# A hybrid decoder trunk in float32 on one core: weight columns streamed from last to first, with two SBUF regions moved by 128 and 256 bytes

## The chip, the cores and the metric

One core of one Trainium2 chip runs the whole program. The metric is the time on the device in microseconds (us) of one execution. Three runs of the kernel before gave 2097.42, 2097.78 and 2098.17 us; the median is 2097.78.

## The reference

Two pre-norm residual layers and a final RMSNorm, on one sequence of 256 rows of 2048 float32 numbers:

```python
h = x
for i in range(2):
    if i == 0: h = h + stick_breaking_mixer(rmsnorm(h, sb_norm), w_qkv, w_o)   # 16 heads of 128
    else:      h = h + chunked_gmlp_mixer(rmsnorm(h, gm_norm), w_in, v_norm, w_s, b_s, w_o)
    gate, up = split(rmsnorm(h, ffn_norm[i]) @ w_gate_up[i])                    # 2048 -> 2 x 5632
    h = h + (silu(gate) * up) @ w_down[i]                                       # 5632 -> 2048
return rmsnorm(h, final_norm)
```

The weights are 2048 x 6144 (qkv), 2048 x 2048 (attention output), 2048 x 4096 (gMLP input), 2048 x 2048 (gMLP output) and, twice, 2048 x 11264 and 5632 x 2048, all float32. Nearly all of the work is in these eight products.

## The kernel before, in words

**Precision.** Each product is made of three: an operand is split into a high part, rounded to the type float32r, and a low part, the difference. TensorE sums high x high, low x high and high x low.

**Pieces.** The weights are cut into pieces of 256 rows (KP = 2 tiles of 128) by 512 columns (CH). There are 752 of them. A piece takes one slot of a ring of four: SP loads it into `raw`, ACT copies it into `w_hi` (line 348), DVE writes raw minus w_hi into `w_lo` (line 654), and PE uses both. Semaphores `raw_loaded`, `hi_ready`, `lo_ready` and `used` hand a slot on. ACT and DVE run LEAD = 3 pieces ahead of PE.

**PE's work on a piece** is in `piece`. The stationary operand of a matmul is a 128 x 128 tile of the transposed activations (`xT`, or `hid_hi` and `hid_lo` in the region that also holds the attention and gMLP buffers); every matmul has its own load of such a tile, listed as PEld. The moving operand is 128 x 512 of `w_hi` or `w_lo`. Two row tiles, two k tiles and two parts give 8 matmuls on `w_hi` (line 1085); then come 4 on `w_lo` (line 1091). The first eight pieces, while the inputs are still being prepared, and the last four, which are taken row tile by row tile, use the order high-high, high-low, low-high instead (lines 1106 to 1108 and 1343 to 1345).

**Accumulator.** `acc` is four banks of PSUM: two halves, used by turns from one column chunk to the next, of two row tiles of 512 float32 columns each. `acc_at(chunk, rt)` gives one of them.

**Order of the stages.** qkv in four rounds of 24 pieces, with the attention of four heads of the round before put between the pieces (`scores`, line 1156, `values`, line 1176, plain float32); the attention output projection; gate and up of the FFN in eleven rounds of 16 pieces; down in four column chunks of 22 pieces; and the same again with the gMLP in the mixer's place, whose mixing matmuls are at line 1302. On PE the later qkv rounds (line 1215), the residual projections (line 1241), gate/up (line 1257) and the gMLP chunks (lines 1287 and 1307) are hardware loops; the down projections are straight code.

**Addresses.** Tensors follow each other in each partition's memory. `lead_in` is padding that puts the start of `region` at a multiple of 512 bytes from `w_hi`; a stationary tile is 512 bytes of a partition, a moving one 2048. `xT`, `w_hi` and `w_lo` lie at multiples of 512 from each other as well, by their sizes.

Of the kernel before, what the change touches and what calls it, by code (L numbers as in the profile page):

```python
# [5 lines left out]
def hybrid_trunk(nc, x, sb_norm, sb_w_qkv, sb_w_o, gm_norm, gm_w_in, gm_v_norm, gm_w_s, gm_b_s, gm_w_o,  # L6
# [19 lines left out]
    P = 128  # L26
    Q = 32
    S, D = x.shape
    RT = S // P
    F = ffn_w_down.shape[1]  # L30
    CH = 512
    KD = D // P
    KF = F // P
    ND = D // CH
# [8 lines left out]
    RING = 4  # L43
# [26 lines left out]
    def half(v):  # L70
        return v % 2

    ctx = ExitStack()
    with ctx:
        def sb(name, shape, dt=f32):
            return ctx.enter_context(nc.sbuf_tensor(name, shape, dt))
# [6 lines left out]
        xT = sb("xT", [P, KD, 2, S], f32r)  # L83
        xT_hi, xT_lo = xT[:, :, 0], xT[:, :, 1]
        raw = sb("raw", [P, RING, KP, CH])
        w_hi = sb("w_hi", [P, RING, KP, CH], f32r)
        w_lo = sb("w_lo", [P, RING, KP, CH], f32r)
        gate = sb("gate", [P, RT, CH])
        res = sb("res", [P, RT, CH])
# [4 lines left out]
        stop = sb("stop", [P, 3 * P])  # L94
# [9 lines left out]


        used_up_to = nc.lookup_mloc(moments).addr + 32
        lead_in = sb("lead_in", [P, (nc.lookup_mloc(w_hi).addr - used_up_to) % CH // 4])
        region = sb("region", [P, 2 * KF * S])
        R0 = nc.lookup_mloc(region).addr
        assert (R0 - nc.lookup_mloc(w_hi).addr) % CH == 0  # L110
        HB = KF * S * 4

        def at(name, offset, shape, dt=f32):
            return nc.alloc_sbuf_tensor_at(name, shape, dt, offset=R0 + offset)

        hid_hi = at("hid_hi", 0, [P, KF, S], f32r)
        hid_lo = at("hid_lo", HB, [P, KF, S], f32r)
# [24 lines left out]
        acc = ctx.enter_context(nc.psum_tensor("acc", [P, 2 * RT * CH], f32))  # L142
# [57 lines left out]
        def acc_at(chunk, rt):  # L200

            return acc[:, bass.ds(half(chunk) * (RT * CH) + rt * CH, CH)]

        def acc_both(chunk):
            return acc[:, bass.ds(half(chunk) * (RT * CH), RT * CH)].rearrange("p (r n) -> p r n", r=RT)
# [134 lines left out]
        def _(act):  # L340
# [47 lines left out]
            def q_or_k(j, sec, dst, done, t_end):  # L388
                act.wait_ge(used, AT_QKV + j * (3 * PD) + t_end)
                if not isinstance(j, int):  # L390
                    act.wait_ge(qk_turned, j * 2 - 1 + sec)
                for r in range(RT):
                    last = nc.scalar.activation(dst[:, r], acc_at(j * 3 + sec, r), ACT.Copy, scale=rstd[:, 0, r:r + 1])
                last.then_inc(done, 1)
# [676 lines left out]
        def _(pe):  # L1071
            def piece(base, it, per, p, chunk, k0, K, hi, lo, first=False):

                if first and p < 2:
                    pe.wait_ge(half_lo, p + 1)
                elif first:
                    pe.wait_ge(lo_ready, base + it * per + p + 1)
                else:
                    pe.wait_ge(hi_ready, base + it * per + p + 1)
                    for k in range(KP):  # L1080
                        kt = k0 + k
                        for r in range(RT):
                            rs = slice(r * P, (r + 1) * P)
                            for part in (hi, lo):
                                nc.tensor.matmul(acc_at(chunk, r), part[:, kt, rs], w_hi[:, p % RING, k],  # L1085
                                                 start=(kt == 0 and part is hi), stop=False)
                    pe.wait_ge(lo_ready, base + it * per + p + 1)
                    for k in range(KP):
                        kt = k0 + k
                        for r in range(RT):  # L1090
                            last = nc.tensor.matmul(acc_at(chunk, r), hi[:, kt, r * P:(r + 1) * P],  # L1091
                                                    w_lo[:, p % RING, k], start=False, stop=(kt == K - 1))
                    last.then_inc(used, 1)
                    return
                for k in range(KP):
                    kt = k0 + k
                    if first:
                        if p == 0 and k == KP // 2:
                            turn_x0(1, x0_rest_loaded)
                        if p < 2 and k == KP // 2:  # L1100
                            pe.wait_ge(lo_ready, p + 1)
                        pe.wait_ge(n_lo[0], kt + 1)
                    for r in range(RT):
                        rs = slice(r * P, (r + 1) * P)
                        dst = acc_at(chunk, r)
                        nc.tensor.matmul(dst, hi[:, kt, rs], w_hi[:, p % RING, k], start=(kt == 0), stop=False)  # L1106
                        nc.tensor.matmul(dst, hi[:, kt, rs], w_lo[:, p % RING, k], start=False, stop=False)  # L1107
                        last = nc.tensor.matmul(dst, lo[:, kt, rs], w_hi[:, p % RING, k], start=False,  # L1108
                                                stop=(kt == K - 1))
                last.then_inc(used, 1)  # L1110

# [20 lines left out]
            def turn_x0(u, loaded):  # L1132
                pe.wait_ge(loaded, 16)
                for k in (2 * u, 2 * u + 1):
                    for r in range(RT):
                        last = nc.tensor.transpose(tp[0][:, k * S + r * P:k * S + (r + 1) * P],  # L1136
                                                   h[:, r, k * P:(k + 1) * P], ident[:, :])
                last.then_inc(n_turned[0], 1)
# [48 lines left out]
            def first_round():  # L1187
                for t, (sec, p) in enumerate(FIRST):
                    if sec == 2 and p == 0:
                        pe.wait_ge(q_out, 1)  # L1190
                    piece(AT_QKV, 0, 3 * PD, t, sec, p * KP, KD, xT_hi, xT_lo, first=sec == 0)
                    if t < 2:
                        turn_x(1 + t)
                    if t == 5:
                        pe.wait_ge(rows_loaded, 4 * 16)
                        turn_rows(tp[0][:, 0:4 * KD], rows, 4 * KD)

            def qkv_round(j):
                for sec in range(3):
                    for p in range(PD):  # L1200
                        t = sec * PD + p
                        if p == 0:

                            pe.wait_ge((k_out, v_out, q_out)[sec], j + (1 if sec == 2 else 0))
                        piece(AT_QKV, j, 3 * PD, t, j * 3 + sec, p * KP, KD, xT_hi, xT_lo)
                        attention(j - 1, t)
# [5 lines left out]
            turn_x0(0, x_loaded[0])  # L1212
            warm_up(4)
            first_round()
            with pe.Fori(1, ND) as j:
                qkv_round(j)


# [19 lines left out]
            turn(tp[0], res).then_inc(n_turned[1], 1)  # L1238

            def residual_rest(which, base, hi, lo, first):  # L1240
                with pe.Fori(first, ND) as c:
                    for p in range(PD):
                        piece(base, c, PD, p, c, p * KP, KD, hi, lo)
                    pe.wait_ge(res_ready[which], c)
# [23 lines left out]
            for it in range(ND // 2):  # L1268
                for t in range(2 * PF):
                    p = t % PF  # L1270
# [10 lines left out]
            for t, (c, p) in enumerate(PAIR):  # L1281
# [2 lines left out]
                if c == 1 and p == 0:  # L1284
                    pe.wait_ge(res_ready[1], ND)
                piece(AT_GMI, 0, 2 * PD, t, c, p * KP, KD, xT_hi, xT_lo)
            with pe.Fori(2, ND) as c:
                pe.wait_ge(gelu_ready, c - 1)
                for p in range(PD):
                    piece(AT_GMI, c, PD, p, c, p * KP, KD, xT_hi, xT_lo)  # L1290
# [13 lines left out]
                        last.then_inc(mixed_ready, 1)  # L1304

            u_chunk(0, True)
            with pe.Fori(1, ND) as c:
                u_chunk(c, False)
            pe.wait_ge(gelu_ready, 2 * ND - 1)
            for p in range(PD):  # L1310
# [10 lines left out]
            for it in range(ND // 2):  # L1321
                for t in range(2 * PF if it == 0 else ROWWISE):
                    p = t % PF
# [10 lines left out]
            it = ND // 2 - 1  # L1334
            for r in range(RT):
                rs = slice(r * P, (r + 1) * P)
                dst = acc_at(1, r)
                for t in range(ROWWISE, 2 * PF):
                    if r == 0:
                        pe.wait_ge(lo_ready, AT_DOWN[1] + it * (2 * PF) + t + 1)  # L1340
                    for k in range(KP):
                        kt = (t - PF) * KP + k
                        nc.tensor.matmul(dst, hid_hi[:, kt, rs], w_hi[:, t % RING, k], start=False, stop=False)  # L1343
                        nc.tensor.matmul(dst, hid_hi[:, kt, rs], w_lo[:, t % RING, k], start=False, stop=False)  # L1344
                        last = nc.tensor.matmul(dst, hid_lo[:, kt, rs], w_hi[:, t % RING, k], start=False,  # L1345
                                                stop=(kt == KF - 1))
                    if r == RT - 1:
                        last.then_inc(used, 1)
                    elif t == 2 * PF - 1:
                        last.then_inc(first_rows, 1)  # L1350
# [28 lines left out]
```

## Time and profile before

| | |
|---|---|
| median of three runs | 2097.78 us |
| span of the profiled execution | 2097.8 us |
| PE busy | 2088.2 us, 100% |
| PEld busy | 1729.4 us |
| DVE busy | 1430.7 us, 68% |
| ACT busy | 1013.1 us, 48% |
| moved by DMA | 402.47 MB, 192 GB/s on average |

PE is TensorE's matmul side and PEld its loads of stationary tiles, which run beside the matmuls. Matmuls overlap in the pipeline: each is listed with about 0.39 us, so what tells the rate is the difference between two starts, not the duration. The clock granted to TensorE is given as a share of 2.4 GHz.

### The profile page before, as it was taken

The page shows a single profiled execution, that of the slowest core. Times are in us where ns is not written, and L with a number is a line of the kernel's source. Part 1 is how long each engine was busy: PE and PEld are TensorE (multiplying, and loading weights), DVE is VectorE, ACT ScalarE, POOL GpSimd, SP SyncE. Part 2 cuts the span into 40 slices and gives each one's busy share as a digit, 9 for nine tenths or more (in the row PEclk, how much of TensorE's full clock was granted, in tenths as well). Part 3 has the DMA queues.
Part 4 walks back from the last instruction along what each step waited for, and adds up shares of the span by engine and source line. Part 5 has one row for each costly group of instructions (what it writes and reads, how often), then busy time and mean ns, then how long its engine had stood idle before and what let it go on. Part 6 is the DMA issues. An engine that isn't in the chain of part 4 may idle for free.

```text
span 2097.8 us, 27159 instructions
## 1 busy us (share of the span) xinstructions
PE 2088.2 (100%) x9281; PEld 1729.4 (82%) x9281; DVE 1430.7 (68%) x1822; ACT 1013.1 (48%) x1285; POOL 16.4 (1%) x30
## 2 busy tenths in 40 slices
PE   9999999999999999999999999999999999999998
PEld 7888888888888888888888888888888888888887
DVE  6787777867666676665557887877666676664444
ACT  6577765544444444444445444554444444444443
POOL 1000000000000000000000000000000000000000
PEclk9999999999999999999999999999999999999999
DMA  8555554666666666555566665566666666655554
GB/s 264 179 179 170 181 189 167 198 196 192 191 190 198 191 193 195 192 191 196 194 192 209 190 200 183 190 190 201 192 189 198 192 193 194 190 194 198 192 191 150
DMA packets 207419, 402.47 MB, mean 192 GB/s; under 512 B 12336, under 2 KB 13056, under 8 KB 206976
## 3 DMA queue, kind: packets, MB, share of 16 engines
q1 hardware_dynamic: 206496, 398.11, 61.1%
q0 software_dynamic: 688, 3.18, 0.4%
q8 instruction: 36, 0.59, 0.1%
q10 hardware_dynamic: 176, 0.40, 0.1%
q14 instruction: 23, 0.19, 0.0%
HBM read 399.55 MB, written 2.10 MB: 191 GB/s over the span
## 4 chain that ended last, share of the span: by engine, by line
PE 99%; issue 0%; DMA 0%; DVE 0%; ACT 0%; POOLq 0%; POOL 0%; DVEq 0%; SPq 0%
PE acc L1085 64%; PE acc L1091 32%; PE tp L1156 0%; PE tp L1176 0%; PE acc L1106 0%; PE acc L1107 0%; PE acc L1108 0%; PE tp L1302 0%; DMA h<-in_x 0%; PE tp L1116 0%; PE acc L1345 0%; PE acc L1344 0%; PE acc L1343 0%; PE acc L1143 0%; PE tp L1136 0%
## 5 line engine op out<-in xcount | busy, mean ns | idle before, releaser
L654 DVE TENSOR_TENSOR w_lo<-raw,w_hi 128x1024 fp32r<-128x1024 f32 x750 | 916.0, 1224 | 584.9 <-ACT w_hi L348 581.1
L348 ACT ACTIVATE w_hi<-raw 128x1024 fp32r<-128x1024 f32 x750 | 792.9, 1060 | 922.4 <-PE acc L1091 917.2
L1085 PE MATMUL acc<-w_hi,xT 128*128 128x512 f32 x4032 | 998.7, 390 | 0.0
L1085 PEld LDWEIGHTS acc<-w_hi,xT 128*128 128x128 f32 x4032 | 756.0, 188 | 155.9
L1091 PE MATMUL acc<-w_lo,xT 128*128 128x512 f32 x2016 | 539.2, 389 | 0.0
L1091 PEld LDWEIGHTS acc<-w_lo,xT 128*128 128x128 f32 x2016 | 378.6, 188 | 78.5
L1085 PE MATMUL acc<-w_hi,hid_hi 128*128 128x512 f32 x944 | 368.7, 391 | 0.0
L1085 PE MATMUL acc<-w_hi,hid_lo 128*128 128x512 f32 x944 | 367.6, 389 | 0.0
L1091 PE MATMUL acc<-w_lo,hid_hi 128*128 128x512 f32 x944 | 252.5, 389 | 0.0
L1091 PEld LDWEIGHTS acc<-w_lo,hid_hi 128*128 128x128 f32 x944 | 177.3, 188 | 36.7
L1085 PEld LDWEIGHTS acc<-w_hi,hid_hi 128*128 128x128 f32 x944 | 177.3, 188 | 36.8
L1085 PEld LDWEIGHTS acc<-w_hi,hid_lo 128*128 128x128 f32 x944 | 177.3, 188 | 36.4
L853 DVE STREAM_TRANSPOSE tp<-res 32x256 f32<-32x256 f32 x352 | 160.5, 456 | 7.9
L691 DVE STREAM_TRANSPOSE tp<-res 32x256 f32<-32x256 f32 x224 | 102.1, 456 | 4.5
L426 ACT ACTIVATE probT<-prob_blk 32x96 f32<-32x96 f32 x192 | 50.1, 261 | 29.2 <-DVE prob_blk L759 27.0
L533 ACT ACTIVATE gate<-acc,rstd 128x512 f32<-128x512 f32 x44 | 27.9, 685 | 33.2 <-PE acc L1091 33.2
L843 DVE SCALAR_TENSOR_TENSOR res<-acc,rstd,gate 128x512 f32<-128x512 f32 x44 | 31.0, 747 | 9.8 <-PE acc L1091 9.8
L733 DVE STREAM_TRANSPOSE k_t<-k_s 32x256 f32<-32x256 f32 x64 | 27.8, 435 | 1.2
L733 DVE STREAM_TRANSPOSE q_t<-q_s 32x256 f32<-32x256 f32 x64 | 27.9, 435 | 1.2
L862 DVE TENSOR_TENSOR hid_lo<-tp,hid_hi 128x1024 f32 (+1 forms) x22 | 26.8, 1218 | 0.0
L358 ACT ACTIVATE xT<-tp,cols 128x256 fp32r<-128x256 f32 (+1 forms) x48 | 18.9, 475 | 10.1 <-DVE tp L691 10.0
L745 DVE TENSOR_TENSOR_SCAN left<-keep,stop 128x384 f32<-128x384 f32 x16 | 15.3, 955 | 12.0 <-ACT take L410 12.0
(115 smaller groups left out, 477.6 us busy)
## 6 DMA issues: line engine op xcount, KB each, us to landing
raw<-in_ffn_w_gate_up SPq DMA_DIRECT2D x352, 512.0 KB, 4.5
raw<-in_ffn_w_down SPq DMA_DIRECT2D x176, 512.0 KB, 3.6
raw<-in_sb_w_qkv SPq DMA_DIRECT2D x95, 512.0 KB, 4.3
raw<-in_gm_w_in SPq DMA_DIRECT2D x64, 512.0 KB, 4.4
raw<-in_sb_w_o SPq DMA_DIRECT2D x32, 512.0 KB, 4.1
raw<-in_gm_w_o SPq DMA_DIRECT2D x32, 512.0 KB, 4.0
h<-in_x SPq DMA_DIRECT2D x3, 512.0 KB, 7.6
gain_bc<-in_gm_v_norm POOLq DMA_DIRECT2D x1, 1024.0 KB, 6.1
```

The source lines that it names most:

```text
L348: nc.scalar.activation(w_hi[:, p % RING], raw[:, p % RING], ACT.Copy).then_inc(hi_ready, 1)
L358: last = nc.scalar.activation(tile(xT_hi, c * TC + k), tp[0 if m or half(c) == 0 else 1][:, k * S:(k + 1) * S], ACT.Copy, scale=cols[:, ba ...
L426: last = nc.scalar.activation(dst[b * Q:(b + 1) * Q, ns, a], src[a * Q:(a + 1) * Q, ns, b], ACT.Copy)
L533: last = nc.scalar.activation(gate[:, r], acc_at(0, r), ACT.Silu, scale=rstd[:, 1 + 2 * layer, r:r + 1])
L654: nc.vector.tensor_tensor(w_lo[:, p % RING], raw[:, p % RING], w_hi[:, p % RING].bitcast(f32), ALU.subtract).then_inc(lo_ready, 1)
L691: last = nc.vector.transpose(tp[0][b * Q:(b + 1) * Q, :].rearrange("p (k r q t) -> p k r q t", k=TC, r=RT, q=4)[:, :, :, a], res[a * Q:(a ...
L733: last = nc.vector.transpose(dst[b * Q:(b + 1) * Q, :, :].rearrange("p k (r q t) -> p k r q t", r=RT, q=4)[:, :, :, a], src[a * Q:(a + 1) ...
L843: last = nc.vector.scalar_tensor_tensor(out=res[:, r], in0=acc_at(1, r), scalar=rstd[:, 1 + 2 * layer, r:r + 1], in1=gate[:, r], op0=ALU.m ...
L853: last = nc.vector.transpose(tp[1][b * Q:(b + 1) * Q, :].rearrange("p (k r q t) -> p k r q t", k=TC, r=RT, q=4)[:, :, :, a], res[a * Q:(a ...
L862: nc.vector.tensor_tensor(hid_lo[:, ks, :], tp[1][:, :].rearrange("p (k t) -> p k t", k=TC), hid_hi[:, ks, :].bitcast(f32), ALU.subtract). ...
L1085: nc.tensor.matmul(acc_at(chunk, r), part[:, kt, rs], w_hi[:, p % RING, k], start=(kt == 0 and part is hi), stop=False)
L1091: last = nc.tensor.matmul(acc_at(chunk, r), hi[:, kt, r * P:(r + 1) * P], w_lo[:, p % RING, k], start=False, stop=(kt == K - 1))
```

## The change

Every matmul on the weights reads its 512 columns from last to first, and writes the accumulator from last to first. The low ring `w_lo` gets 128 bytes of padding ahead of it (`w_gap`), and `lead_in` puts `region` at 256 bytes past a multiple of 512 from `w_hi`; asserts fix the three distances. The stationary operands are read as before. PE's hardware loops over the later qkv rounds, the residual projections and the gMLP chunks become Python loops, so that PE's code for them is written out; the gate/up loop stays. ACT, DVE, POOL and SP run the same instructions, on the moved addresses.

```diff
         w_hi = sb("w_hi", [P, RING, KP, CH], f32r)
+        w_gap = sb("w_gap", [P, P // 4])
         w_lo = sb("w_lo", [P, RING, KP, CH], f32r)
...
-        lead_in = sb("lead_in", [P, (nc.lookup_mloc(w_hi).addr - used_up_to) % CH // 4])
+        lead_in = sb("lead_in", [P, (nc.lookup_mloc(w_hi).addr + CH // 2 - used_up_to) % CH // 4])
         region = sb("region", [P, 2 * KF * S])
         R0 = nc.lookup_mloc(region).addr
-        assert (R0 - nc.lookup_mloc(w_hi).addr) % CH == 0
+        assert (R0 - nc.lookup_mloc(w_hi).addr) % CH == CH // 2
+        assert (nc.lookup_mloc(xT).addr - nc.lookup_mloc(w_hi).addr) % CH == 0
+        assert (nc.lookup_mloc(w_lo).addr - nc.lookup_mloc(w_hi).addr) % CH == P
...
+        def acc_back(chunk, rt):
+
+            return acc[:, ::-1][:, bass.ds((2 * RT - 1 - rt) * CH - half(chunk) * (RT * CH), CH)]
+
+        def back(t, slot, k):
+
+            return t[:, slot, k, ::-1]
...
-                                nc.tensor.matmul(acc_at(chunk, r), part[:, kt, rs], w_hi[:, p % RING, k],
+                                nc.tensor.matmul(acc_back(chunk, r), part[:, kt, rs], back(w_hi, p % RING, k),
                                                  start=(kt == 0 and part is hi), stop=False)
...
-                            last = nc.tensor.matmul(acc_at(chunk, r), hi[:, kt, r * P:(r + 1) * P],
-                                                    w_lo[:, p % RING, k], start=False, stop=(kt == K - 1))
+                            last = nc.tensor.matmul(acc_back(chunk, r), hi[:, kt, r * P:(r + 1) * P],
+                                                    back(w_lo, p % RING, k), start=False, stop=(kt == K - 1))
...
-            with pe.Fori(1, ND) as j:
+            for j in range(1, ND):
                 qkv_round(j)
...
-                with pe.Fori(first, ND) as c:
+                for c in range(first, ND):
...
-            with pe.Fori(2, ND) as c:
+            for c in range(2, ND):
                 pe.wait_ge(gelu_ready, c - 1)
...
-            with pe.Fori(1, ND) as c:
+            for c in range(1, ND):
                 u_chunk(c, False)
```

The same replacement of `acc_at` by `acc_back` and of the weights by `back(...)` is made in the first round and in the last four pieces.

The order on PE at the start of the later qkv rounds, before: the last piece of the first round and the first two pieces of the loop, with its branch and the instructions that make up its addresses.

```order
L1085 MATMUL acc<-w_hi,xT 128x512 x8
L1091 MATMUL acc<-w_lo,xT 128x512 x4
L1215 UNCONDITIONAL_BRANCH
L1079 ISA
L1085 ISA
L1085 MATMUL acc<-w_hi,xT 128x512 x2
L1085 ISA
L1085 MATMUL acc<-w_hi,xT 128x512 x6
L1091 MATMUL acc<-w_lo,xT 128x512 x4
L1079 REGISTER_ALU
```

And in the changed kernel, PE at the same place: pieces of the second round, up to its first attention step.

```order
L1096 MATMUL acc<-w_hi,xT 128x512 x8
L1102 MATMUL acc<-w_lo,xT 128x512 x4
L1167 MATMUL tp<-kT,qT 128x128
L1167 MATMUL tp<-kT,qT 128x256
L1096 MATMUL acc<-w_hi,xT 128x512 x8
L1102 MATMUL acc<-w_lo,xT 128x512 x4
```

Branch and register instructions are gone from the round; the matmuls and their order are the same (all lines lie 11 further down).

PE at the start of the looped gate/up rounds of the changed kernel:

```order
L1096 MATMUL acc<-w_hi,xT 128x512 x8
L1102 MATMUL acc<-w_lo,xT 128x512 x4
L1268 UNCONDITIONAL_BRANCH
L1090 ISA
L1096 MATMUL acc<-w_hi,xT 128x512 x8
L1102 MATMUL acc<-w_lo,xT 128x512 x4
L1090 REGISTER_ALU
```

This loop stands as before, with one register instruction per piece.

## Rows read from the trace of the kernel before

**Rows 1.** The page: busy us, share of the span, instructions.

```profile
PE 2088.2 (100%) x9281; PEld 1729.4 (82%) x9281; DVE 1430.7 (68%) x1822; ACT 1013.1 (48%) x1285; POOL 16.4 (1%) x30
```

**Rows 2.** Waits of PE: who waited for what, us, times, longest.

```profile
PE acc L1143 <- DVE junk L775: 1.5, 1, 1.5
PE tp L1136 <- DMA h<-in_x: 0.4, 1, 0.4
PE acc L1106 <- DVE w_lo L681: 0.2, 1, 0.2
```

**Rows 3.** Windows: stretch, its length, busy us per engine, clock, DMA share, GB/s.

```profile
887.03:1091.03 204.00, 204.00 (x901) 169.01 (x900) 122.43 (x140) 90.50 (x103) 0.00 (x0) 1.00 0.59 194
```

**Rows 4.** The page: the chain that ended last, by engine.

```profile
PE 99%; issue 0%; DMA 0%; DVE 0%; ACT 0%; POOLq 0%; POOL 0%; DVEq 0%; SPq 0%
```

**Rows 5.** The chain in order of time, gate/up: start us, us, what.

```profile
523.62 1.81 PE acc L1085 x8
...
697.70 1.81 PE acc L1085 x8
```

**Rows 6.** Timeline of PE, attention output projection: start us, us.

```profile
343.04 1.07 PE L1091 MATMUL acc<-w_lo,hid_hi 128*128 128x512 f32 x4
...
356.63 1.07 PE L1091 MATMUL acc<-w_lo,hid_hi 128*128 128x512 f32 x4
```

**Rows 7.** Timeline of PE and PEld, one piece of the down projection.

```profile
1000.14 0.39 PE L1085 MATMUL acc<-w_hi,hid_lo 128*128 128x512 f32 x1
1000.14 0.19 PEld L1085 LDWEIGHTS acc<-w_hi,hid_hi 128*128 128x128 f32 x1
...
1002.86 0.39 PE L1085 MATMUL acc<-w_hi,hid_lo 128*128 128x512 f32 x1
```

**Rows 8.** Timeline of PE, first matmuls of the first round.

```profile
8.70 0.63 PE L1107 MATMUL acc<-w_lo,xT 128*128 128x512 f32 x1
9.13 0.63 PE L1108 MATMUL acc<-w_hi,xT 128*128 128x512 f32 x1
9.55 0.63 PE L1106 MATMUL acc<-w_hi,xT 128*128 128x512 f32 x1
```

**Rows 9.** Timeline of PE, float32 passes of 256 columns in the attention.

```profile
118.21 0.60 PE L1156 MATMUL tp<-kT,qT 128*128 128x256 f32 x2
118.43 0.38 PE L1156 MATMUL tp<-kT,qT 128*128 128x256 f32 x1
118.64 0.38 PE L1176 MATMUL tp<-probT,v_f 128*128 128x256 f32 x1
```

**Rows 10.** Timeline of PE, the piece after an attention step.

```profile
299.07 0.39 PE L1085 MATMUL acc<-w_hi,hid_lo 128*128 128x512 f32 x1
...
300.68 0.62 PE L1091 MATMUL acc<-w_lo,hid_hi 128*128 128x512 f32 x2
```

**Rows 11.** The groups of instructions: the matmuls on the weights, by shape.

```profile
L1085 PE MATMUL acc<-w_hi,xT 128*128 128x512 f32 x4032 | 998.7, 390 | 0.0
L1091 PE MATMUL acc<-w_lo,xT 128*128 128x512 f32 x2016 | 539.2, 389 | 0.0
L1085 PE MATMUL acc<-w_hi,hid_hi 128*128 128x512 f32 x944 | 368.7, 391 | 0.0
L1106 PE MATMUL acc<-w_hi,xT 128*128 128x512 f32 x32 | 13.4, 418 | 0.2 <-DVE w_lo L681 0.2
L1343 PE MATMUL acc<-w_hi,hid_hi 128*128 128x512 f32 x16 | 6.2, 389 | 0.0
```

**Rows 12.** The page: DMA queues, packets, MB, share of 16 engines.

```profile
q8 instruction: 36, 0.59, 0.1%
q14 instruction: 23, 0.19, 0.0%
```

**Rows 13.** Windows of the gate/up stage and the gMLP u half.

```profile
523.62:697.70 174.08, 174.08 (x770) 144.24 (x769) 117.45 (x141) 75.71 (x76) 0.00 (x0) 1.00 0.65 193
1220.00:1290.00 70.00, 70.00 (x337) 58.90 (x336) 62.14 (x109) 30.73 (x33) 0.00 (x0) 1.00 0.57 179
```

More of the change, by code:

```diff
@@ L1104, in piece @@
                         rs = slice(r * P, (r + 1) * P)
[L1105 to L1108, printed above, removed]
+                        dst = acc_back(chunk, r)
+                        nc.tensor.matmul(dst, hi[:, kt, rs], back(w_hi, p % RING, k), start=(kt == 0), stop=False)
+                        nc.tensor.matmul(dst, hi[:, kt, rs], back(w_lo, p % RING, k), start=False, stop=False)
+                        last = nc.tensor.matmul(dst, lo[:, kt, rs], back(w_hi, p % RING, k), start=False,
                                                 stop=(kt == K - 1))
@@ L1336, in _ @@
                 rs = slice(r * P, (r + 1) * P)
-                dst = acc_at(1, r)
+                dst = acc_back(1, r)
                 for t in range(ROWWISE, 2 * PF):
@@ L1342, in _ @@
                         kt = (t - PF) * KP + k
-                        nc.tensor.matmul(dst, hid_hi[:, kt, rs], w_hi[:, t % RING, k], start=False, stop=False)
-                        nc.tensor.matmul(dst, hid_hi[:, kt, rs], w_lo[:, t % RING, k], start=False, stop=False)
-                        last = nc.tensor.matmul(dst, hid_lo[:, kt, rs], w_hi[:, t % RING, k], start=False,
+                        nc.tensor.matmul(dst, hid_hi[:, kt, rs], back(w_hi, t % RING, k), start=False, stop=False)
+                        nc.tensor.matmul(dst, hid_hi[:, kt, rs], back(w_lo, t % RING, k), start=False, stop=False)
+                        last = nc.tensor.matmul(dst, hid_lo[:, kt, rs], back(w_hi, t % RING, k), start=False,
                                                 stop=(kt == KF - 1))
```

## The prediction

> **What bounds the kernel now.** Start with the busy shares of the page: PE, TensorE's matmul side, is busy for 2088.2 us of a span of 2097.8 [rows 1]. A busy matmul engine may still be starved, so the next view is the list of what PE waited for: three waits of 2.1 us in all, by the warm-up, the first transposes and the first round [rows 2]. The granted clock is 1.00 in the wide stretches, which is the 2.4 GHz level, and PE makes up 99% of the chain that ended last [rows 3, 4]. No transfer, no split on ACT or DVE and no semaphore sets the end: it is set by how often TensorE starts a matmul.
>
> So the one number that matters is the spacing of two matmuls. The chain puts a start of an eight-matmul group at 523.62 us and another at 697.70 us [rows 5]; between them lie 64 whole pieces of 12 matmuls (8 with the high weights, 4 with the low), so one piece takes 174.08 / 64 = 2.720 us and one matmul 226.67 ns. The same step shows in the attention output projection, 343.04 to 356.63 us for five pieces [rows 6], and in the first down columns, where twelve matmuls lead from 1000.14 to 1002.86 [rows 7]. The step is the same over high and low weights, over x and hidden activations, and beside a busy DVE or a quiet one.
>
> What could it be? In the first microseconds, before the clock rises, the same matmuls start at 8.70, 9.13 and 9.55 us [rows 8]: 0.425 us apart, and 0.427 is 512 columns at 1.2 GHz, with nothing else. At 2.4 GHz 512 columns are 213.3 ns. The step of 226.67 ns therefore holds **13.3 ns more than the columns**, 32 cycles at 2.4 GHz, paid only at the fast clock. Two rows say that these are no fixed fee of the array. Float32 passes of 256 columns, at two cycles per column also 213.3 ns of array time but with half the bytes per nanosecond, start at 118.21, 118.43 and 118.64 us: 0.215 us each [rows 9]. And just after such passes the main stream is slower than usual: from 299.07 to 300.68 us seven steps take 1.61 us, 0.230 us each, before it falls back to 0.2267 [rows 10]. The same instructions with the same operand shapes thus run at 0.230 or 0.2267, depending on how they stand to something that runs beside them. What runs beside each matmul is the load of the next stationary tile (PEld): it starts within 0.01 us of the matmul and is listed at 0.19 us [rows 7]. It reads 512 bytes of each partition while the matmul reads 2048. My reading, which the trace of before doesn't prove, is that the two reads of the same memory get in each other's way at 2.4 GHz, and that directions and addresses decide how often.
>
> **The change, part by part.** *Descending columns.* All 512-column matmuls on the weights read w_hi and w_lo from last column to first, and write acc from last to first, so the sum lands in the same places. The number is 4032 + 2016 + 3 x 944 + 3 x 32 + 3 x 16 = 9024 [rows 11]. At 226.67 ns they make 2045.4 us; the other 52.4 us (start, transposes, attention, tail) the change doesn't touch. *Addresses.* Before, xT, w_hi, w_lo and the hidden region all begin at the same residue modulo 512. Now w_lo lies 128 and the region 256 bytes off w_hi, xT stays at 0. Every matmul whose next tile comes from xT or from the region, and every one that reads w_lo, meets another relative address; the first kind with w_hi against xT is moved in direction only. *Price of both.* No row shows a descending read. The bounds: the step can't fall under 213.3 ns, a gain of 9024 x 13.3 = 120 us; a step as in the 256-column passes, 215 ns, gives 105 us. Above, the slowest step in the stream is 230 ns: 9024 x 3.3 = 30 us lost. I take **220 ns**, half of the excess gone: the directions change for all matmuls, so if clashes are the cause their number changes everywhere, but w_hi against xT keeps its residue and the offsets are multiples of 128, so I don't expect all of it. That is 9024 x 6.67 = 60.2 us.
>
> The Trainium skill, "TensorE: Matmul & The Clock Gate", section "Step-by-step: what each phase is for", says the reverse of my reading: the streamed operand and the weight load have two independent read ports, and loading the next tile takes no bandwidth from the running matmul. By it addresses and direction would change nothing and the sum would be 0 us. The step of 0.230 against 0.2267 us in one stream [rows 10] speaks against it here. The same page, "Back-to-back issue gap", gives N / 2.4 + 2.5 ns, 215.8 ns for 512 columns; by it the end would be some 98 us earlier if nothing clashed.
>
> *Loops written out.* PE's loops over the later qkv rounds, the two residual projections and the two gMLP halves become straight code; the gate/up loop of the FFN, the longest, stays a hardware loop. A loop costs nothing today: the pieces with register arithmetic in the loop at 343 us [rows 6], those of the looped gate/up stage [rows 5] and those of the down projection, which was straight code already [rows 7], all take 2.72 us. More code must be fetched: the instruction queues move 0.59 and 0.19 MB now, at 0.1% of the DMA time [rows 12]; even twice that would be small beside the 0.65 that the weights take [rows 13]. Cost 0, covered by a straight-code stage that shows no gap today; if that cover failed, one hole of a microsecond at each written-out round would be some 15 us.
>
> *ACT, DVE, DMA.* They do the same work 3% faster per piece. In the gate/up stretch DVE is busy 117.5 of 174 us, ACT 75.7, and the DMA share is 0.65 [rows 13]: they have room. The narrow place is the gMLP u half, DVE 62.1 of 70 us [rows 13]. At a step of 220 ns these 70 us become 68, DVE's share 0.91: still under the span, though a group that bunches may stop PE for a moment; I book 0. At 215 ns it would be 0.935. DVE's low split reads w_hi and writes w_lo, now 128 bytes apart in residue; if it slowed a little, PE wouldn't see it outside that stage. The adds, the norm and the store behind the last matmul are the same work as before.
>
> Sum: 2097.8 - 60.2 + 0 + 0 = **2037.6 us**. The profiled execution's span, 2097.8 us, and the median of the runs, 2097.78, are the same, so nothing is added. About 0.2%, 4 us, is what a measurement can tell from no change.
>
> **Rivals.** *Nearly all of the excess goes.* If the new directions and residues leave no clash, the step is the 215 ns of the 256-column passes [rows 9]: 2097.8 - 105 = 1993 us. For it: three residues are set with care so that no stationary tile meets w_lo at a difference of 0. Against: w_hi on xT, 4032 of 9024 matmuls, keeps its residue. *Nothing changes.* If the 13.3 ns are a fee of reading four bytes per cycle at 2.4 GHz, direction and residue are beside the point: 2098 us. For it: the piece is 2.72 us in stages with different operands. Against: the 0.230 us steps. *Slower: descending reads keep the stream in the bad phase.* The place is every matmul of the main stream, the mechanism that of [rows 10]: today the stream slips from 0.230 to 0.2267 within eight matmuls. With both streams' relative motion and residues changed it may settle at the slow step, price 3.3 ns each: 2097.8 + 30 = 2128 us. It decides as soon as the mean step is over 226.67 ns. For it: today's residues are all equal, and a step that is common to all operands may be the good one; three of the four pairs of operands leave it. Against: nothing in the trace says that equal residues are best. *Far slower: a descending write costs double.* If each column written or read downwards took two cycles, the step would be that of the slow clock, 427 ns [rows 8]: 9024 x 0.427 + 52 = 3900 us. The Trainium skill, "Advanced Engine Details and Errata", section "PSUM Cachelines", has a rule that points there: any non-contiguous pattern in PSUM slows matmuls much. Nothing in this trace shows such a write; two neighbours still follow each other, only in the other order, so I give it little.
>
> **How the numbers follow.** Half of the excess gone, 2037.6 us: 0.36. Nearly all gone, 1993: 0.20. No change: 0.17. Slower at 2128 or thereabouts: 0.22. Far slower: 0.05. Faster by over 0.2% is 0.36 + 0.20 = 0.56, the same 0.17, slower 0.22 + 0.05 = 0.27. The range reaches from 1992 to 2130 us: it takes in the 215 ns step below and the 230 ns step above, and leaves out the far slower case, the half of the slower case that costs more than one such step, and what lies between 213 and 215 ns, 0.2 together. The likeliest case's own range is 2011 to 2074 us, steps of 217 to 224 ns (9.67 and 2.67 ns times 9024).
>
> **What would show it.** In the changed kernel's chain the piece of 12 matmuls reads 2.64 us in all stages if I am right, 2.72 with no change, 2.58 if all goes, 2.76 in the slower case. If the residues matter, x stages and hidden stages will differ, or the four matmuls on w_lo will differ from the eight on w_hi; if only the direction matters, all are alike. Loops written out show as no gap at the start of a round. A wait of PE on DVE's low split in the gMLP half would show the one place where the cover is thin. I am wrong if the step is unchanged, or if a wait of PE longer than a microsecond takes back what the step gives.

## The result and the profile after

The changed kernel takes 2167.05 us (median; 2166.87 to 2167.41), the kernel before 2097.82 in the same comparison. The ratio is 1.0329, 95% interval 1.0315 to 1.0344: **69 us slower**. I had forecast 2037.6 us and a range that ended at 2130.

The page of the changed kernel (its lines lie 11 further down), answering to [rows 1] and [rows 4]:

```profile
PE 2155.4 (100%) x9281; PEld 1729.6 (80%) x9281; DVE 1430.9 (66%) x1822; ACT 1011.8 (47%) x1285; POOL 16.5 (1%) x30
...
PE 99%; DMA 0%; issue 0%; SPq 0%; DVE 0%; ACT 0%; POOLq 0%; POOL 0%; DVEq 0%
```

Its waits of PE, against [rows 2]: who waited for what, us, times, longest.

```profile
PE acc L1154 <- DVE junk L786: 1.5, 1, 1.5
PE tp L1127 <- DMA h<-in_x: 0.8, 1, 0.8
PE acc L1117 <- DVE xT L684: 0.4, 1, 0.4
```

Nothing starves TensorE, as before: all 67 us of PE's added busy time are its own. DVE, ACT and PEld have the busy time that they had, only their shares fall. The chain in order of time, in the gate/up stage, against [rows 5]:

```profile
521.17 1.87 PE acc L1096 x8
523.04 0.94 PE acc L1102 x4
523.98 1.87 PE acc L1096 x8
...
695.59 1.87 PE acc L1096 x8
```

From 521.17 to 695.59 us are 62 pieces: 2.813 us each where [rows 5] have 2.720, that is 234.4 ns a matmul for 226.7. The eight matmuls on w_hi take 1.87 us for 1.81, the four on w_lo 0.94 for 0.91. The windows of the changed kernel (columns as in [rows 3]) show the clock at its upper level and room beside PE:

```profile
521.17:700.00 178.83, 178.83 (x764) 143.34 (x764) 116.66 (x140) 75.54 (x76) 0.00 (x0) 1.00 0.64 186
1000.00:1100.00 100.00, 100.00 (x428) 80.19 (x427) 63.44 (x78) 44.66 (x54) 0.00 (x0) 1.00 0.59 187
```

And PE's timeline at the last matmul:

```profile
2156.96 0.40 PE L1356 MATMUL acc<-w_hi,hid_lo 128*128 128x512 f32 x1
2157.19 0.40 PE L1354 MATMUL acc<-w_hi,hid_hi 128*128 128x512 f32 x1
...
2157.66 0.40 PE L1356 MATMUL acc<-w_hi,hid_lo 128*128 128x512 f32 x1
```

From here to the end of the span there are 8 us, as there were before. Below, "step" is the time from the start of a piece to the start of the next, divided by 12, averaged over all pieces that directly follow each other (484 with xT, 227 with the hidden region). By that measure the kernel before has 227.1 ns in either kind of stage, and the changed kernel 234.8; a few pieces, most of them behind an attention step or its like, hold a longer gap between two starts, which is why both lie some 0.4 ns above a quiet stretch. The difference, 7.7 ns, times 9024 matmuls is 69 us: the whole loss is in the step. (The expectations below put the changed kernel at 234.6 ns, an average without its longest pieces.)

One rival can be dropped by the traces alone. While the last pieces are computed no transfer is running: the DMA share is 0.00 from 2078 to 2088 us before and from 2147 to 2157 us in the changed kernel. The last 48 matmuls still come 226.7 and 233.4 ns apart. So DMA traffic makes neither the step of before nor the direction's part of the loss.

### The profile page after: what moved, and what is told of

Its sections match the earlier page's. It is cut to its first block, busy times and chain, and to the rows that moved or that the text cites. A ratio compares the mean times of both kernels' runs of the same rounds, so it can differ in the third digit from the quotient of the medians.

```text
span 2165.7 us, 26903 instructions
## 1 busy us (share of the span) xinstructions
PE 2155.4 (100%) x9281; PEld 1729.6 (80%) x9281; DVE 1430.9 (66%) x1822; ACT 1011.8 (47%) x1285; POOL 16.5 (1%) x30
## 4 chain that ended last, share of the span: by engine, by line
PE 99%; DMA 0%; issue 0%; SPq 0%; DVE 0%; ACT 0%; POOLq 0%; POOL 0%; DVEq 0%
PE acc L1096 64%; PE acc L1102 32%; PE tp L1167 0%; PE tp L1187 0%; DMA h<-in_x 0%; PE tp L1313 0%; PE acc L1117 0%; PE acc L1118 0%; PE acc L1119 0%; PE tp L1127 0%; PE acc L1356 0%; PE acc L1355 0%; PE acc L1354 0%; PE tp L1175 0%; SPq L228 0%
## 5 line engine op out<-in xcount | busy, mean ns | idle before, releaser
L1096 PE MATMUL acc<-w_hi,xT 128*128 128x512 f32 x4032 | 1025.9, 398 | 0.0
L1102 PE MATMUL acc<-w_lo,xT 128*128 128x512 f32 x2016 | 558.2, 399 | 0.0
L1096 PE MATMUL acc<-w_hi,hid_lo 128*128 128x512 f32 x944 | 375.8, 398 | 0.0
L1096 PE MATMUL acc<-w_hi,hid_hi 128*128 128x512 f32 x944 | 375.4, 398 | 0.0
L1102 PE MATMUL acc<-w_lo,hid_hi 128*128 128x512 f32 x944 | 261.4, 399 | 0.0
L550 ACT ACTIVATE hid_hi<-tp 128x1024 f32 (+1 forms) x22 | 22.5, 1025 | 0.0
```

The lines of the kernel that those rows point to most:

```text
L550: nc.scalar.activation(hid_hi[:, bass.ds(i * TC, TC), :], tp[1][:, :].rearrange("p (k t) -> p k t", k=TC), ACT.Copy).then_inc(f_hi[layer], 1)
L1096: nc.tensor.matmul(acc_back(chunk, r), part[:, kt, rs], back(w_hi, p % RING, k), start=(kt == 0 and part is hi), stop=False)
L1102: last = nc.tensor.matmul(acc_back(chunk, r), hi[:, kt, r * P:(r + 1) * P], back(w_lo, p % RING, k), start=False, stop=(kt == K - 1))
```

## The experiments

A residue is the distance of a buffer's start from that of w_hi, modulo 512 bytes. Three theories go into the first runs: D, the descending direction costs it; A, the moved addresses do; M, both act together. Later S says that the distance between a weight operand and the stationary tile that is loaded beside it counts, and L that it is the distance between w_hi and w_lo.

The first three runs were timed four to ten times each and spread by under 1 us. The runs from e4 on were timed once each; the kernel before, timed beside them, took 2097.4 to 2097.9 us. The losses and gains that are read from them against the kernel before are 29 us and more.

### The change taken apart

**e1_dir_only**: the changed kernel with the old addresses.

```diff
-        w_gap = sb("w_gap", [P, P // 4])
...
-        lead_in = sb("lead_in", [P, (nc.lookup_mloc(w_hi).addr + CH // 2 - used_up_to) % CH // 4])
+        lead_in = sb("lead_in", [P, (nc.lookup_mloc(w_hi).addr - used_up_to) % CH // 4])
```

> The changed kernel with the addresses of the kernel before: w_lo, xT and the region all at residue 0 from w_hi, columns and accumulator still descending, loops written out. Theory D (the descending direction alone costs the step, addresses are idle): the step over a piece stays at 234.6 ns and the time at 2167 us. Theory A (the moved addresses alone cost it): the step falls to 227.1 ns and the time to 2098 us. Theory M (direction and addresses act together, each direction has its own good residues): the time differs from both, above 2167 us if 0 is a bad residue for descending reads (240 ns, 2215 us), between the two if it is a good one.

Measured: 2157.13 us, ratio 1.0284 (1.0266 to 1.0301), step 233.7 ns in both kinds of stage. Direction alone costs 59 of the 69 us; the addresses add 10.

**e2_offsets_only**: the kernel before with the new addresses.

```diff
+        w_gap = sb("w_gap", [P, 32])
         w_lo = sb("w_lo", [P, RING, KP, CH], f32r)
...
+        lead_in = sb("lead_in", [P, (nc.lookup_mloc(w_hi).addr + 256 - used_up_to) % CH // 4])
```

> The kernel before with the two moved addresses (w_lo 128 bytes, the region 256 bytes off), columns ascending, loops as before. Theory D: 2098 us, step 227.1 ns. Theory A: 2167 us, 234.6 ns. Theory M: slower than before, as equal residues are then the good ones for ascending reads; the four matmuls on w_lo and the hidden stages would show it, the eight on w_hi in the x stages not.

Measured: 2131.09 us, ratio 1.0158 (1.0141 to 1.0175), step 230.8 ns with xT and 230.9 with the region. Without the direction the addresses cost 33 us. 59 and 33 don't add up to 69: theory M. But stages with the region at 256 and those with xT at 0 take the same, which none of the theories said. Nor do the eight matmuls on w_hi in the stages with xT keep their step, as M had it: in quiet pieces they take 230.1 ns, where the kernel before has 226.7.

**e3_loops_only**: the kernel before with the loops written out.

```diff
-            with pe.Fori(1, ND) as j:
+            for j in range(1, ND):
```

(and the same for the other three loops of the change)

> The kernel before with PE's loops over the later qkv rounds, the residual projections and the gMLP chunks written out, nothing else. All theories: 2098 us within 0.2%. A rival in which code fetch costs a part of the loss: over 2102 us, with gaps on PE at the rounds that are written out.

Measured: 2097.86 us, ratio 1.0000 (0.9991 to 1.0010). Written-out loops are free, although the instruction queue moves more, here in the page of the changed kernel (packets, MB, share; [rows 12] have 0.59 MB):

```profile
q8 instruction: 46, 0.75, 0.2%
```

**e4_read_only**: the changed kernel, with the accumulator written upwards.

```diff
-                                nc.tensor.matmul(acc_back(chunk, r), part[:, kt, rs], back(w_hi, p % RING, k),
+                                nc.tensor.matmul(acc_at(chunk, r), part[:, kt, rs], back(w_hi, p % RING, k),
```

> The changed kernel with the weights read from last to first but the accumulator written from first to last, so each sum lands in the mirrored column: the output is not the reference's. It separates the read of SBUF from the write of PSUM. If the descending read carries the cost, the step stays 234.6 ns and the time 2167 us; if the descending write of the accumulator does, 227.1 ns and 2098 us.

Measured: 2166.75 us, step 234.8 ns in both kinds of stage: as the changed kernel. The descending read of SBUF carries the cost. A descending write of PSUM adds nothing to a stream that is already held up by its reads.

### Which distance counts

**e6_lo_128**: the kernel before with `w_gap` of 128 bytes alone.

> The kernel before with w_lo 128 bytes off, the region left at residue 0, columns ascending. Theory L (the distance between the two rings of moving operands counts, stationary tiles don't): as with both offsets, 2131 us and 230.8 ns a matmul, in x stages and hidden stages alike. Theory S (the distance between a moving operand and the tile that is loaded beside it counts): the hidden stages lose less or more than the x stages, since the region is back at 0. Theory R (the region's 256 bytes are the cost): 2098 us.

Measured: 2130.87 us, 230.8 and 230.9 ns, as e2. The region's 256 bytes cost nothing; the 128 bytes of w_lo are the whole cost of the addresses. Theory R is out; L fits so far.

**e7_fwd_tiles**: the kernel before, tiles moved against the weights.

```diff
+        x_gap = sb("x_gap", [P, 16])
         w_hi = sb("w_hi", [P, RING, KP, CH], f32r)
...
+        lead_in = sb("lead_in", [P, (nc.lookup_mloc(w_hi).addr + 32 - used_up_to) % CH // 4])
```

> The kernel before with only the stationary tiles moved against the weights: xT 64 bytes off w_hi and w_lo, the region 32 bytes off, w_hi and w_lo at equal residues, columns ascending. Theory L: 2098 us, 227.1 ns in both kinds of stage. Theory S: both kinds of stage change, and by different amounts (each some ns up, as 0 was the chosen residue): over 2110 us.

Measured: 2129.62 us; 229.3 ns in the stages with xT, 233.7 in those with the region. The chain of this kernel, gate/up (xT 64 below the weights) and then down (region 32 above):

```profile
530.10 1.83 PE acc L1087 x8
531.93 0.92 PE acc L1093 x4
532.85 1.83 PE acc L1087 x8
```

```profile
940.69 1.87 PE acc L1087 x8
942.55 0.93 PE acc L1093 x4
943.49 1.87 PE acc L1087 x8
```

In the first stretch a piece takes 2.75 us, in the second 2.80; the instructions have the same form, the distance of the tile differs. With w_hi and w_lo at equal residues L forecast 2098 us and falls; **S holds for ascending reads**. S alone does not give e6, though. There the tile lies at 0 for the eight matmuls on w_hi and 128 below for the four on w_lo. With the steps that the table below has for these two distances an estimate is 229.0 ns, about 17 us lost; measured were 230.8 ns and 33 us, and the matmuls on w_hi were slower too. A stream that changes its distance within each piece loses more than its distances one by one; why was not tested.

**e8_back_tiles**: the same distances with descending reads (x_gap 64 bytes, region 32, w_lo at 0, `back` and `acc_back` kept).

> The changed kernel with w_lo back at residue 0, xT 64 bytes and the region 32 bytes off the weights, columns descending. Theory L: as in the run with all residues 0, 2157 us and 233.7 ns in both kinds of stage. Theory S: the two kinds of stage differ from 233.7 ns and from each other; one of them may fall below it, which would show that descending reads want another distance.

Measured: 2157.04 us, 233.7 ns in both kinds of stage, as with all residues 0 (e1). With w_hi and w_lo at equal residues a descending read takes the same step at all three distances tried (0, 192 and 32, modulo 256). S doesn't hold there.

**e12_fwd_scan, e13_fwd_scan, e18_fwd_scan**: ascending, with other gaps (`x_gap` of 128, 32 and 192 bytes; region at 192, 96 and 160).

> Ascending columns, w_hi and w_lo at equal residues, xT 128 bytes below a multiple of 512 from them and the region 192 above, that is 64 below modulo 256. If the distance between tile and weights counts modulo 256, the hidden stages take 229.3 ns, as the x stages did with xT 64 below; with another period something else. The x stages at 128 below have no forecast but that they are over 226.7 ns if equal residues are the best.

> Ascending columns, w_hi and w_lo at equal residues, xT 32 bytes below them and the region 96 above. It looks for a distance that beats 0. Theory S: both kinds of stage differ from 227.1 ns, and the time lies between 2098 and 2160 us; a step under 226.7 ns in either would be a version to put together.

> Ascending columns, w_hi and w_lo at equal residues, xT 192 bytes below them, that is 64 above modulo 256, and the region 160 above. These are the two distances in steps of 32 bytes that were not measured. If 0 is the best distance, both kinds of stage take more than 227.1 ns, most likely 230 to 235; a step below 227.1 in either would beat the kernel before.

Measured: 2138.90, 2158.88 and 2156.56 us. With e7 and the kernel before, the steps for ascending reads, w_hi and w_lo at equal residues, are:

| tile above the weights, bytes modulo 256 | step, ns | from |
|---|---|---|
| 0 | 227.1 | before |
| 32 | 233.7 | e7, region |
| 64 | 233.7 | e18, xT |
| 96 | 234.7 | e13, region |
| 128 | 232.8 | e12, xT |
| 160 | 233.7 | e18, region |
| 192 | 229.3 and 229.4 | e7, xT; e12, region |
| 224 | 233.7 | e13, xT |

The two entries at 192 come from an xT that lies 64 below the weights and from a region that lies 192 above them: they agree, and 0 and 128 do not, which fits a period of 256 bytes and rules out 128 bytes or a smaller part of it. That is also why the region's move by 256 did nothing. Of the eight, 0 is the best, and it is what the kernel before had.

### What it is in the read

**e10_still_fwd and e11_still_back**: each stationary tile is its first column, read 128 times; ascending (on e3) and descending (on e1).

```diff
+        def still(t):
+
+            return t[:, 0:1].to_broadcast([P, P])
```

> The kernel before with PE's loops written out (which costs nothing) and each stationary tile replaced by its first column, read 128 times: the load has as many columns, but reads a single address of each partition, so the products are rank one and the output is not the reference's. Columns of the weights ascending. Theory C (the 13.3 ns above the 213.3 ns of the columns are clashes of the matmul's read with the tile load's read of other addresses): the step falls, to about 215 to 220 ns, 1995 to 2040 us. Theory F (they are a fee of the moving read itself): 227 ns, 2098 us. A load that hammers one address could also clash more than one that walks: then the step rises.

> The same replacement in the kernel with descending columns and all residues 0 (2157 us, 233.7 ns). Output not the reference's, as above. Theory C: direction costs only through the clash with the tile load, so both directions now take the same step as in the ascending run beside this one. Theory F2 (a descending read is dearer by itself): the step stays 6.5 ns above that of the ascending run.

Measured: 2127.40 us, 230.5 ns with xT and 230.4 with the region ascending; 2157.10 us and 233.7 ns descending. Holding the load on one address gains nothing, so C's number did not come, and F's did not either: for an ascending read a still tile is better than six of the eight distances and worse than 0. The descending read keeps its step. That is not F2, which asked for 6.5 ns above the ascending run and got 3.3: only the ascending step had moved.

**e15_still_weights**: the other side held still, each weight operand being its first column, read 512 times.

```diff
-            return t[:, slot, k, ::-1]
+            return t[:, slot, k, 0:1].to_broadcast([P, CH])
```

> All residues 0, loops written out, accumulator ascending; each moving operand is its first column, read 512 times, so TensorE streams 512 columns but reads one address of each partition, and the output is not the reference's. If the 13.3 ns above the 213.3 ns of the columns come from walking through the memory beside the tile load, the step falls to about 215 ns, 1993 us. If they are a fee of the matmul itself, it stays at 227 ns. If staying on one address is bad in itself, it rises.

Measured: 2021.22 us, step 218.1 and 218.2 ns. The chain of this kernel in the gate/up stage:

```profile
527.42 1.74 PE acc L1094 x8
529.17 0.87 PE acc L1100 x4
530.04 1.74 PE acc L1094 x8
```

In the last four pieces 48 matmuls come 215.8 ns apart, where the kernel before has 226.7. So **9 to 11 of the 13.3 ns above the columns are the price of walking** through the weights, paid by the kernel before as well; some 2 to 5 ns are left with a read that stays on one address. This run does not say what the walk meets: with the tile still and the weights walking (e10) nothing was gained.

**e16_blocks_16B, e17_blocks_256B and e19_blocks_128B**: the columns are taken in blocks from last to first, ascending inside each; 4, 64 and 32 columns a block, read and written alike, all residues 0.

```diff
-            return t[:, slot, k, ::-1]
+            return t[:, slot, k].rearrange("p (b c) -> p b c", c=64)[:, ::-1]
```

> All residues 0, loops written out; the 512 columns are taken in blocks of 4 (16 bytes) from the last block to the first, but ascending inside a block, in the read and in the accumulator alike. If the dearer step comes from the order inside 16 bytes, it falls to 227 ns, 2098 us. If it comes from the order in which the 16-byte blocks are walked, it stays at 233.7 ns, 2157 us. If it comes from the walk over longer stretches, it stays too.

> The same with blocks of 64 columns (256 bytes, the period that the distances between tile and weights showed), descending from block to block and ascending inside. If what counts is how the two reads move against each other inside the 256-byte period, the step is that of ascending reads, 227 ns and 2098 us. If any descending step costs, it lies at or near 233.7 ns, 2157 us.

> All residues 0, blocks of 32 columns (128 bytes) from last to first, ascending inside. With blocks of 256 bytes the step was that of ascending reads, with blocks of 16 bytes that of descending ones. If the period that counts is 256 bytes, half of it is walked in the wrong order and the step lies over 227.1 ns (229 to 234); if it is 128 bytes or less, it is 227.1 ns.

Measured: 2157.14, 2097.84 and 2148.16 us; steps 233.7, 227.1 and 232.7 ns with xT. The chain of the kernel with 256-byte blocks:

```profile
524.56 1.81 PE acc L1094 x8
526.38 0.91 PE acc L1100 x4
527.28 1.81 PE acc L1094 x8
```

and with 128-byte blocks, the eight matmuls of a piece on w_hi:

```profile
524.61 1.86 PE acc L1094 x8
527.40 1.86 PE acc L1094 x8
530.19 1.86 PE acc L1094 x8
```

Walking down costs nothing when each stretch of 256 bytes is walked up: the kernel is as fast as the one before. Order inside 16 bytes makes no difference: blocks of 16 bytes cost as much as single columns. Blocks of 128 bytes taken downwards visit the two halves of each 256 bytes in exchanged order, so at any moment the read stands where an ascending read at a distance of 128 would, modulo 256; and the steps of both are the same, 232.7 ns with xT here and 232.8 in the table (232.4 for both in quiet pieces). What counts is **where in 256 bytes the read stands at each moment**, not the direction as such.

**e14_light_splits**: the changed kernel, with ACT and DVE splitting 64 of 512 columns after the first round.

```diff
+                cs = slice(0, CH if base == 0 and isinstance(it, int) and it == 0 else CH // 8)
+                nc.scalar.activation(w_hi[:, p % RING, :, cs], raw[:, p % RING, :, cs], ACT.Copy).then_inc(hi_ready, 1)
```

(and the same for DVE's subtraction)

> The changed kernel (descending, w_lo 128 and the region 256 bytes off), where after the first round of pieces ACT and DVE split only 64 of the 512 columns of each weight tile; the rest of w_hi and w_lo keeps what the first pieces left, so the output is not the reference's. It takes most of the two engines' traffic away. If the 0.9 ns by which the moved w_lo makes the descending step longer (234.6 against 233.7 ns) are clashes with the writes and reads of the splits, the step falls to 233.7 ns or under; if they are not, it stays at 234.6 ns. The part of the loss that is the direction's, 6.5 ns, stays in either case unless the splits cause that as well.

Measured: 2166.87 us, 234.8 ns in both kinds of stage, with DVE busy for 758.4 us where the changed kernel has 1430.9, and ACT for 475.7 where it has 1011.8. Neither the direction's 6.6 ns nor the 1.1 ns of w_lo come from the traffic of the splits.

## Why the prediction was wrong, point by point

- **What bounds the kernel** held: TensorE is never starved, and the time moved by the step alone, 7.7 ns on 9024 matmuls.
- **The 13.3 ns above the columns are clashes of the two reads** is borne out in part. They are no fixed fee: with the weights held still the step is 218.1 ns, and 215.8 in the tail, about the 215 of the 256-column passes that I had set beside it. That a distance can decide was right too: 227.1 ns at 0, up to 234.7 elsewhere. That the 13.3 ns paid at distance 0 come from the tile's load is not shown; a still tile did not take them away. The statement of the Trainium skill ("TensorE: Matmul & The Clock Gate", "Step-by-step: what each phase is for") that a tile load takes nothing from the running matmul does not hold for this stream: e7 differs from the kernel before only in the distance between tiles and weights and is 32 us slower.
- **The step that failed is "I take 220 ns, half of the excess gone".** It was a middle between the floor of 213 ns and today's step, held up by "if clashes are the cause their number changes everywhere", which says nothing of the sign. The runs showed 234.8 ns in its place: the step rose by 7.7 ns and did not fall by 6.7. The step of before already was the best of eight distances. The descending read alone took it to 233.7 ns, +6.6, and w_lo's 128 bytes added 1.1.
- **Descending is indifferent to the distance.** I let w_hi on xT, with its residue kept, pass for the least affected pair. At descending reads the distances 0, 192 and 32 and a still tile all give 233.7 ns, so that pair paid like the others.
- **The offsets** gave 33 us on their own and 10 beside the direction, all of them by w_lo. The region's 256 bytes did nothing: I had read residues modulo 512, as the assert of the kernel writes them, and the table repeats at 256.
- **The slower rival** had the right sign and place, and its argument came true: "today's residues are all equal, and a step that is common to all operands may be the good one". Its price, 3.3 ns, was mis-sized: I took the slowest step that [rows 10] showed in the stream, 230 ns, for an upper bound. Those rows are seven steps of a stream that returns to 226.7 ns, and no bound for another walk through the memory. Measured: 7.7 ns. For the same reason the range ended at 2130. Whether the slow moment of [rows 10] and the descending step have one cause is not shown; a quiet stretch of the changed kernel has 234.4 ns and not 230.
- **Far slower through PSUM** did not come. The rule of the Trainium skill ("Advanced Engine Details and Errata", "PSUM Cachelines") that a non-contiguous pattern slows matmuls does not reach a descending one here: with and without the descending write the step is 234.8 ns, and with blocks of 64 columns downwards 227.1. A fully descending write beside a read at 227 ns was not run.
- **Loops written out, ACT, DVE and DMA at nothing**: right, with a ratio of 1.0000 for the loops alone. Of the forecasts on the profile, a piece of 2.76 us was the nearest to the 2.81 that came, and the matmuls on w_lo do differ from those on w_hi: 236.5 against 233.4 ns in quiet pieces.

**Open.** Why a descending read takes 233.7 ns at every distance tried, while the ascending one has a good place, was not shown. The picture of two reads, of tile and weights, that meet in parts of a 256-byte stretch fits the table and the blocks, but a still tile should then have changed the descending step, and didn't. Nor is the 1.1 ns settled by which w_lo at 128 makes the descending step longer. Nearly all of it is in the four matmuls on w_lo (236.5 ns, in e1 233.3), and it is not the splits' traffic. In the last four pieces it is gone: the changed kernel has 233.4 ns and e1 233.3. There high and low operands alternate and no transfer is running, and no run tells which of the two matters; the distance alone does not make it. Distances other than multiples of 32 bytes, and walks other than blocks downwards, were not tried. No version ran faster than the kernel before with its work complete.

## What to carry to other kernels

When TensorE is busy all the time, take the difference of two starts, far apart, and compare it with the columns at the granted clock: here 13.3 of 226.7 ns were no columns, and 9 to 11 of them went with the walk through the weights. Before changing addresses or directions in such a stream, vary one distance in two stages of one run and look at the step of each; a stream whose operands all share a residue may owe its speed to that. And the slowest step seen in a stream is no ceiling for what a change can cost.

## What the runs showed of the hardware

- Float32r matmuls of 512 columns at 2.4 GHz, each with its own tile load, take between 227.1 and 234.7 ns with the distance between moving and stationary operand modulo 256 bytes (before, e7, e12, e13, e18), 230.5 ns with a tile of one address (e10), and 218.1 ns with a moving operand of one address (e15).
- Descending columns take 233.7 ns at every distance tried while w_hi and w_lo share a residue (e1, e8), and 234.8 with w_lo 128 bytes off (the changed kernel). Descending blocks of 128 bytes, ascending inside, take 232.7 ns (e19), of 256 bytes 227.1 (e17).
- The order inside 16 bytes did not matter at 233.7 ns (e16), nor the order of the columns in PSUM at 234.8 (e4).
- Writing out PE's loops over rounds and chunks cost nothing: 2097.86 us against 2097.83 (e3).
